# Gathering the experts' tokens from the fp32 stream, with a tenth expert unit loaded ahead

## What is computed

```python
h = layer_norm(DEEPNORM_ALPHA * h + mix, ln1_g[i], ln1_b[i])
...
t = h.reshape(b * l, d)
group_probs = jax.nn.softmax((t @ router_group_w).astype(jnp.float32) + router_group_b, axis=-1)
g_idx = jnp.argmax(group_probs, axis=-1)
exp_logits = jnp.einsum("td,gde->tge", t, router_expert_w).astype(jnp.float32) + router_expert_b
...
for gi in range(N_GROUPS):
    hid = (jax.nn.silu(jnp.einsum("td,edf->tef", t, expert_w_gate[gi]))
           * jnp.einsum("td,edf->tef", t, expert_w_up[gi]))
    hid = hid * combine[:, gi, :, None].astype(hid.dtype)
    y = y + jnp.einsum("tef,efd->td", hid, expert_w_down[gi])
```

## Time and profile before

| | us |
|---|---|
| median of 3 runs | 1086.28 |
| lowest, highest | 1086.09, 1087.94 |
| the profiled execution | 1088.23 |
| its span, first to last instruction | 1086.1 |
| PE busy in the span | 983.1 (91%) |
| DVE, ACT busy | 498.5 (46%), 354.2 (33%) |
| mean granted TensorE clock (share of full speed) | 0.964 |

### The profile page before, as it was taken

One profiled execution on the slowest core, in us unless ns is written; L12 is line 12 of the kernel. 1 busy time (PEld: TensorE's weight loads), 2 busy tenths in 40 slices (PEclk: granted clock), 3 DMA queues, 4 the chain that ended last, 5 costly groups with the idle time before them and its releaser, 6 DMA issues.

```text
span 1086.1 us, 14285 instructions
## 1 busy us (share of the span) xinstructions
PE 983.1 (91%) x6105; PEld 726.6 (67%) x6105; DVE 498.5 (46%) x777; ACT 354.2 (33%) x456; POOL 33.8 (3%) x51
## 2 busy tenths in 40 slices
PE   8989989999999984656877999999999989999996
PEld 7988776444456432213336887599998879889995
DVE  5973563271246102001038446355656565655554
ACT  3555303841022110001025436134343334434341
POOL 1400100021000000000000000000000000000000
PEclk9989999999999997878999999999999999999999
DMA  9724420452942999999995460445545344545520
GB/s 334 218 86 148 147 88 1 155 184 97 415 156 100 417 421 421 421 421 421 422 396 189 156 227 5 155 155 191 197 164 222 118 154 155 213 175 198 189 77 39
DMA packets 67126, 229.38 MB, mean 211 GB/s; under 512 B 4080, under 2 KB 5392, under 8 KB 54400
## 3 DMA queue, kind: packets, MB, share of 16 engines
q1 hardware_dynamic: 65216, 223.28, 54.2%
q0 software_dynamic: 1632, 5.26, 1.3%
q10 hardware_dynamic: 224, 0.07, 0.0%
HBM read 227.54 MB, written 1.05 MB: 210 GB/s over the span
## 4 chain that ended last, share of the span: by engine, by line
PE 74%; DMA 12%; DVE 9%; issue 2%; SPq 2%; ACT 1%; DVEq 0%; ACTq 0%
PE bank L1253 17%; PE bank L1264 16%; PE bank L1036 5%; DMA ring<-in_expert_w_up 5%; PE bank L676 4%; DMA arena<-in_expert_w_up 3%; PE bank L1162 3%; PE bank L665 3%; PE bank L960 3%; PE bank L929 3%; PE bank L1229 3%; PE bank L652 2%; DMA arena<-in_expert_w_down 2%; DVE arena L1744 2%; PE bank L1167 2%
## 5 line engine op out<-in xcount | busy, mean ns | idle before, releaser
L2174 DVE TENSOR_TENSOR w_lo<-ring,w_hi 128x2048 fp32r<-128x2048 f32 x76 | 170.6, 2288 | 97.4 <-ACT w_hi L1556 97.4
L1556 ACT ACTIVATE w_hi<-ring 128x2048 fp32r<-128x2048 f32 x76 | 141.1, 1909 | 87.9 <-PE bank L1264 86.9
L1253 PE MATMUL bank<-xT_hi,w_hi 128*128 128x256 f32 x512 | 143.8, 281 | 2.6 <-DVE xT_lo L2162 2.6
L1253 PE MATMUL bank<-xT_hi,w_lo 128*128 128x256 f32 x512 | 143.6, 280 | 0.0
L1253 PE MATMUL bank<-xT_lo,w_hi 128*128 128x256 f32 x512 | 143.2, 280 | 0.0
L1264 PE MATMUL bank<-w_hi,hidden_lo 128*128 128x512 f32 x256 | 99.9, 390 | 0.0
L1264 PE MATMUL bank<-w_lo,hidden_hi 128*128 128x512 f32 x256 | 99.8, 390 | 0.0
L1264 PE MATMUL bank<-w_hi,hidden_hi 128*128 128x512 f32 x256 | 99.6, 389 | 0.0
L1253 PEld LDWEIGHTS bank<-xT_hi,w_hi 128*128 128x128 f32 x512 | 96.1, 188 | 3.5 <-issue 3.0
L1253 PEld LDWEIGHTS bank<-xT_lo,w_hi 128*128 128x128 f32 x512 | 96.4, 188 | 0.5
L1253 PEld LDWEIGHTS bank<-xT_hi,w_lo 128*128 128x128 f32 x512 | 95.9, 187 | 0.0
(11 more groups left out here) (489 smaller groups left out, 1621.5 us busy)
## 6 DMA issues: line engine op xcount, KB each, us to landing
ring<-in_mlp_w_up SPq DMA_DIRECT2D x32, 1024.0 KB, 6.6
ring<-in_mlp_w_down SPq DMA_DIRECT2D x32, 1024.0 KB, 6.3
ring<-in_w_in SPq DMA_DIRECT2D x22, 1024.0 KB, 7.6
ring<-in_expert_w_down SPq DMA_DIRECT2D x22, 1024.0 KB, 19.7
ring<-in_expert_w_gate SPq DMA_DIRECT2D x16, 1024.0 KB, 15.4
ring<-in_expert_w_up SPq DMA_DIRECT2D x16, 1024.0 KB, 17.4
arena<-in_expert_w_gate SPq DMA_DIRECT2D x15, 1024.0 KB, 12.8
arena<-in_expert_w_up SPq DMA_DIRECT2D x15, 1024.0 KB, 14.8
```

The lines of the kernel that those rows point to most:

```text
L1253: last = mm(B[4 + (2 * j + pr) % 4][:, cc * SEQ:(cc + 1) * SEQ], w_[:, k * 512 + c * P:k * 512 + (c + 1) * P], x_[:, k, 0:SEQ], start=(k = ...
L1556: act(whi[:, n % 2, half], slot(u)[:, half], ACT.Copy).then_inc(S("split_hi"), 1)
L2174: tt(wlo[:, u % SLOTS, half], slot(u)[:, half], f32(whi[:, n % 2, half]), ALU.subtract).then_inc(S("split_lo"), 1)
```

## The change

- The gather reads X0 itself, in fp32, through a view with a step of 8 elements (`xhatT`); `hiX`, `loX`, `rounded`, `low_part` and the wait for `h1_low` are gone. `sel` and `sel_spill` are plain fp32. Of the matmuls in each gather 16 fp32 ones are left, with the same columns.
- A third unit is loaded once: unit 1 now takes all of X1, unit 2 lies in X2 and the start of `xT` and waits for the last output projection. All later units move down by one slot. Units 0 to 9 are now loaded ahead; unit j waits for unit j - 7 from j = 10 on.
- One `keep_going(1)` (an fp32 product of 512 columns whose result nobody reads) ahead of the rank products is removed.
- In a fallback for more overfull experts, which these inputs don't enter, X1 takes X0's place (that part of the diff is left out here).

```diff
--- before.py
+++ after.py
@@ -225,13 +225,10 @@
     wr, rbias = cube(arena[:, 18496:18496 + KD * 36], KD), arena[:, 18784:18820]
-    hiX = parts("h1_hi", "X1", 0, NT * D).rearrange("p (i k c) -> p i k c", i=NT, k=KD)
-    loX = parts("h1_lo", "xT", 0, NT * D).rearrange("p (i k c) -> p i k c", i=NT, k=KD)
+    xhatT = X0[:, :, :].rearrange("p i (c k) -> p i k c", k=KD)
     taken["arena"] = 0
-    sel = cube(parts("select", "arena", 0, NT * PAIR), NT)
-    reg(NT * PAIR)
-    sel_spill = cube(parts("select_spill", "arena", taken["arena"], NT * SPILL), NT)
-    reg(NT * SPILL)
+    sel = cube(reg(NT * PAIR), NT)
+    sel_spill = cube(reg(NT * SPILL), NT)
     selw = cube(reg(NT * PAIR), NT)
     selw_spill = cube(reg(NT * SPILL), NT)
     xs = cube(reg(KD * PAIR), KD)
@@ -327,20 +324,22 @@
     FIRST = MOE_UNITS + 2
     SPILLED = QUADS
     ORDER = [0, 1, SPILLED] + list(range(2, QUADS))
-    once = (params[:, :, :].rearrange("p a d -> p (a d)"), nc.alloc_sbuf_tensor_at("X1_X2", [P, UNIT], F32, offset=placed["X1"] + 4 * NT * D)[:, :])
+    ONCE = 3
+    assert placed["xT"] == placed["X2"] + 4 * NT * D == placed["X1"] + 4 * 3 * NT * D
+    once = [params[:, :, :].rearrange("p a d -> p (a d)"), X1[:, :, :].rearrange("p a d -> p (a d)"), nc.alloc_sbuf_tensor_at("X2_xT", [P, UNIT], F32, offset=placed["X2"])[:, :]]
     spare = [arena[:, SPARE + a * UNIT:SPARE + (a + 1) * UNIT] for a in range(3)]
-    FIRST_USE = [0, 5, 6, 7, 8, 2, 1, 3, 4]
+    FIRST_USE = [0, 5, 6, 7, 8, 9, 1, 3, 2, 4]
     def moe_at(s_, j):
         if s_ is None:
-            return MOE_SLOTS + j if j < 2 else (j - 2) % MOE_SLOTS
+            return MOE_SLOTS + j if j < ONCE else (j - ONCE) % MOE_SLOTS
         return j % MOE_SLOTS
     def moe_slot(s_, j):
         m = moe_at(s_, j)
-        return once[m - MOE_SLOTS] if m >= MOE_SLOTS else spare[m - 3] if 3 <= m < 6 else ring[:, {6: 3}.get(m, m), :]
+        return once[m - MOE_SLOTS] if m >= MOE_SLOTS else spare[m - 2] if 2 <= m < 5 else ring[:, (m + 1) % MOE_SLOTS if m < 2 else 3 * (6 - m), :]
     def moe_unit(s_, q):
@@ -491,17 +490,19 @@
             if s_ is not None:
                 sp.wait_ge(S("moe_unit"), total(s_, FIRST, MOE_UNITS, max(0, j - MOE_SLOTS + 1)))
-            elif j >= MOE_SLOTS + 2:
+            elif j >= MOE_SLOTS + ONCE:
                 sp.wait_ge(S("moe_unit"), j - MOE_SLOTS + 1)
             elif j == 0:
                 sp.wait_ge(S("gate_out"), 8)
                 sp.wait_ge(S("stream_made"), 2)
             elif j == 1:
                 sp.wait_ge(S("four_psum"), 4)
+            elif j == 2:
+                sp.wait_ge(S("mixed"), 4)
             elif j in (5, 6, 7):
                 sp.wait_ge(S("mix_psum"), 4)
             else:
-                of = U_TWO - 4 + (8, 2, 3, 4).index(j)
+                of = U_TWO - 4 + (8, 9, 3, 4).index(j)
                 sp.wait_ge(S(freed[of][0]), freed[of][1])
             for a, src in loads:
                 sp.dma_start(moe_slot(s_, j)[:, a:a + src.shape[1]], src).then_inc(S(f"moe_in{moe_at(s_, j)}"), 16)
@@ -514,7 +515,7 @@
                 flag = sp.value_load(ovi[0:1, 0:1], min_val=0, max_val=1)
                 expert = sp.value_load(ovi[0:1, 1:2], min_val=0, max_val=NG * NE - 1)
             for part in range(6 if q < SPILLED else 2):
-                if moe_unit(None, q) + part > MOE_SLOTS + 1:
+                if moe_unit(None, q) + part >= MOE_SLOTS + ONCE:
                     moe_load(None, moe_unit(None, q) + part, moe_loads(q, part) if q < SPILLED else spill_loads(expert, part))
         with sp.If(flag):
             with sp.Fori(0, PASSES - 1) as s_:
@@ -979,7 +980,6 @@
         carry(1)
         pe.wait_ge(S("router_dve"), 1)
         carry(0)
-        keep_going(1)
         pe.wait_ge(S("router_dve"), 3)
         of = lambda i: member[:, i].rearrange("p g e -> p (g e)")
         mm(B[4][:, 0:32], C("strict"), of(0), start=True, stop=True)
@@ -1001,8 +1001,7 @@
                     gathered(s_, gather_index(s_, p, 0))
                 for kk in range(2):
                     for i in range(NT):
-                        for m, x_ in enumerate((hiX, loX)):
-                            last = mm(B[(5, 6, 7, 5)[b]][:, kk * PAIR:(kk + 1) * PAIR], x_[:, i, 2 * b + kk, :], sel[:, i, :], start=(i == 0 and m == 0), stop=(i == NT - 1 and m == 1))
+                        last = mm(B[(5, 6, 7, 5)[b]][:, kk * PAIR:(kk + 1) * PAIR], xhatT[:, i, 2 * b + kk, :], sel[:, i, :], start=(i == 0), stop=(i == NT - 1))
                 last.then_inc(S("xs_psum"), 1)
         def gather_spill():
@@ -1011,8 +1010,7 @@
             for n in range(2):
                 for c in range(4):
                     for i in range(NT):
-                        for m, x_ in enumerate((hiX, loX)):
-                            last = mm(B[6 + n][:, c * P:(c + 1) * P], x_[:, i, 4 * n + c, :], sel_spill[:, i, :], start=(i == 0 and m == 0), stop=(i == NT - 1 and m == 1))
+                        last = mm(B[6 + n][:, c * P:(c + 1) * P], xhatT[:, i, 4 * n + c, :], sel_spill[:, i, :], start=(i == 0), stop=(i == NT - 1))
                 last.then_inc(S("xs_psum"), 1)
         def moe_landed(s_, j):
@@ -1020,8 +1018,8 @@
             m = moe_at(s_, j)
             if m >= MOE_SLOTS:
                 return pe.wait_ge(S(f"moe_in{m}"), 32)
-            main, per = 32 * len(range(m + 2, FIRST, MOE_SLOTS)), 32 * len(range(m, MOE_UNITS, MOE_SLOTS))
-            pe.wait_ge(S(f"moe_in{m}"), total(s_, main, per, 32 * ((j - (2 if s_ is None else 0)) // MOE_SLOTS + 1)))
+            main, per = 32 * len(range(m + ONCE, FIRST, MOE_SLOTS)), 32 * len(range(m, MOE_UNITS, MOE_SLOTS))
+            pe.wait_ge(S(f"moe_in{m}"), total(s_, main, per, 32 * ((j - (ONCE if s_ is None else 0)) // MOE_SLOTS + 1)))
         def up_quad(s_, q):
@@ -1130,7 +1128,6 @@
                     down_quad(s_, q)
             scatter(s_, order[-1], False, True)
-        pe.wait_ge(S("h1_low"), 2)
         keep_going(1)
         experts(None, ORDER)
         pe.wait_ge(S("over_made"), 1)
@@ -1486,18 +1483,11 @@
         warm_sqrt()
         deviation(5, slice(1, 3))
-        def rounded(i):
-
-            sc.wait_ge(S("xhat"), i + 1)
-            act(hiX[:, i], X0[:, i, :].rearrange("q (p k) -> q k p", k=KD), ACT.Copy).then_inc(S("h1_round"), 1)
-
-        rounded(0)
         for b in (0, 2):
             sc.wait_ge(S("four_psum"), 4 + b + 1)
             for k in (2 * b, 2 * b + 1):
                 last = act(xs[:, k, :], B[4 + b][:, (k % 2) * SEQ:(k % 2 + 1) * SEQ], ACT.Identity, scale=by_feature["ln1_g"][:, k:k + 1], bias=by_feature["ln1_b"][:, k:k + 1])
             last.then_inc(S("turned_act"), 1)
-        rounded(1)
         sc.wait_ge(S("router_dve"), 2)
         act(gd, gd, ACT.Exp).then_inc(S("router_act"), 1)
         sc.wait_ge(S("router_dve"), 4)
@@ -1948,13 +1938,6 @@
                 last = ts(xs[:, k, :], B[4 + b][:, (k % 2) * SEQ:(k % 2 + 1) * SEQ], by_feature["ln1_g"][:, k:k + 1], by_feature["ln1_b"][:, k:k + 1], ALU.mult, ALU.add)
             last.then_inc(S("turned_dve"), 1)
-        def low_part(i):
-
-            dve.wait_ge(S("xhat"), i + 1)
-            dve.wait_ge(S("h1_round"), i + 1)
-            tt(loX[:, i], X0[:, i, :].rearrange("q (p k) -> q k p", k=KD), f32(hiX[:, i]), ALU.subtract).then_inc(S("h1_low"), 1)
-
-        low_part(0)
         dve.wait_ge(S("router_in"), 16 * (NG + 5))
         dve.wait_ge(S("router_psum"), 1)
         for i in range(NT):
@@ -1987,7 +1970,6 @@
         line(tt(both, oh1, oh2, ALU.add))
         spread = lambda out, vals: [tt(out[:, i], oh[:, i, :].unsqueeze(2).broadcast_to([P, NG, NE]), vals[:, i, :].unsqueeze(1).broadcast_to([P, NG, NE]), ALU.mult) for i in range(NT)][-1]
         spread(member, both).then_inc(S("router_dve"), 1)
-        low_part(1)
         line(tt(w2, top2, top1, ALU.subtract))
         dve.nop().then_inc(S("router_dve"), 1)
         dve.wait_ge(S("router_dve"), 3)
@@ -2008,7 +1990,7 @@
             dve.wait_ge(S("sel_made"), pair_made(s_, p))
             for i in range(NT):
                 w_ = weight[:, i].rearrange("p g e -> p (g e)")[:, 8 * p:8 * p + 8].unsqueeze(2).broadcast_to([P, 8, CAP])
-                last = tt(cube(selw[:, i, :], 8), cube(f32(sel[:, i, :]), 8), w_, ALU.mult)
+                last = tt(cube(selw[:, i, :], 8), cube(sel[:, i, :], 8), w_, ALU.mult)
             last.then_inc(S("sel_weighed"), 1)
         select(0)
@@ -2062,7 +2044,7 @@
         red(spill_w, tmp, AX.X, ALU.add).then_inc(S("weighed"), 1)
         dve.wait_ge(S("weighed"), 2)
         for i in range(NT):
-            last = ts(selw_spill[:, i, :], f32(sel_spill[:, i, :]), spill_w[:, i:i + 1], None, ALU.mult)
+            last = ts(selw_spill[:, i, :], sel_spill[:, i, :], spill_w[:, i:i + 1], None, ALU.mult)
         last.then_inc(S("sel_weighed"), 1)
         def quad(s_, q):
```

6 lines of the change are left out of this document (3 added, 3 removed).

## The result

| | before | after |
|---|---|---|
| median of 5 runs, us | 1087.94 | 1093.16 |
| lowest, highest | 1086.09, 1089.28 | 1092.90, 1093.83 |
| span of the profiled execution, us | 1086.1 | 1091.1 |

The ratio is 1.005, with an interval of 1.0038 to 1.0063: slower by 5.2 to 5.4 us. I had forecast 1090.4 us, that is 4.1 us slower on a median of 1086.28, and a range up to 1092.6. The direction and the mechanism were right.

What follows compares the result with a forecast made beforehand. The expert stage was taken as bound by its weight transfers. Shift of first down products, -1.6 + 3.33 + 3.53 = +5.26 us, less 1.14 slack, gives +4.1 on 1086.28: 1090.4 us, range 1086.0 to 1092.6.

Steps and rivals of the forecast that it cites:

- The gap and the slack: Transfers ahead of unit 11: the tenth unit's lead becomes a gap; the stage's end shifts as first down products, less 1.14 us.
- later waits don't bind: Expert stage behind unit 11: unit 13 and later units find enough transfers queued, 10 to 15 us, to cover their waits.
- Slow load against free step: PE's weight loads in both gathers: the 32-byte step slows them (1090.4 us, chance 0.50) or costs nothing (1086.6 us, 0.38).
- The size of the load: Both gathers: a stepped load takes 0.225 us (bounds 0.20 to 0.26), adding 3.33 us to the gather, 3.53 to the spill gather.
- The saving ahead of the gather: Router's end: without the rounded and low parts and one `keep_going`, the path ahead of the gather is 1.6 us shorter.
- The base: Whole time: the 4.1 us shift is added to a median of 1086.28 us, 1.95 us below the profiled execution.
- Half clock: Third rival: a half-clock stretch of about 3.4 us on the gather or spill gather adds 1.7 us, 1092.1 us; chance 0.06.
- Free step: First rival: the step costs PE's weight load nothing, spill gather 3.7 us, 1086.6 us in all; chance 0.38.
- Faster: Second rival: both gathers cost no more than now, leaving saving and slack, -2.7 us, 1083.5 us; chance 0.06.

Runs made afterwards that it cites:

- e1: The changed kernel, but the gather reads the stream's features at a step of 1 element instead of 8 (wrong feature order): 1086.03 us, ratio 0.9984.
- e3: The changed kernel, but the gather reads at a step of 2 fp32 elements (8 bytes) instead of 8 (wrong feature order): 1087.29 us, one execution.
- e11: The changed kernel's fp32 gather with nine units loaded ahead, both gathers reading side by side one fp32 copy that ACT writes in the weights' order: 1089.7 us, ratio 1.0014.
- e10: The changed kernel with the spill gather moved from ahead of the first down products to just ahead of the spilled expert's up products: 1095.77 us, ratio 1.0073.
- e2: The changed kernel's fp32 stepped gather, but with the nine units loaded ahead and the slots of the kernel before: 1093.04 us, ratio 1.0045.
- e9: The kernel before without the `keep_going` ahead of the ranks; ACT scales the transposed stream first, GpSimd makes both low parts: 1089.69 us, ratio 1.0016.

## Why the prediction was too low

| counted from the end of the output projection, us | before | after | e1 | e3 | e11 | e10 |
|---|---|---|---|---|---|---|
| first down products end | 39.60 | 45.96 | 41.05 | 41.26 | 41.04 | 39.38 |
| last unit lands | 236.38 | 241.57 | 236.86 | 237.06 | 237.9 (estimate) | 243.14 |
| last scatter ends | 244.73 | 251.61 | 245.20 | 245.40 | 247.64 | 251.49 |

**The gap and the slack: right.** "Shift of the end = shift of those products - 1.14 us" gives +5.22 for the changed kernel, and +5.19 was measured; +0.31 and +0.52 for e1 and e3, measured +0.48 and +0.68. It fails for e10, where the first down products are no longer what is late. My sentence that "later waits don't bind" was right for this change, whose transfers run on at 418 to 424 GB/s from 384 to 412 us, and no more: it was worked out for PE's order as it stood, and e10 changes that order.

**Slow load against free step: right, by analogy with two other engines.** ACT's and DVE's rows did tell what PE does. The Trainium skill's SBUF — State Buffer, section Specifications (TRN2), asks for two accesses to a line of 16 bytes; steps of 4 and 8 bytes have them and cost next to nothing, 16 and 32 have not and cost double: the traces agree. The Trainium skill's TensorE: Matmul & The Clock Gate, section LDWEIGHTS, gives the time by the columns alone, and no step above 8 bytes here agrees with it.

**The size of the load: the first of two terms that failed.** "I take twice, 0.225 us with a little for the hand-over." The rows of the spill gather's products after:

```profile
L1013 PE MATMUL bank<-arena,X x32: 401/402/502, 346.7 to 354.2; 128*128 128x128 f32 x32
```

With the last one's 0.40 us off, (7.83 - 0.40) / 31 = 0.240 us from load to load, 2.2 times the 0.110 us without a step. That is 0.015 us in each of 62 intervals, 0.93 us. Another 0.33 us lies in the first and last records, which grew too: I had kept 0.38 and 0.28 us. So the gather cost +4.02 instead of +3.33 and the spill gather +4.10 instead of +3.53, together 1.26 us more than the sum had. The 0.240 lay inside my bounds, 0.20 to 0.26.

**The saving ahead of the gather: right.** 1.6 was taken, with 1.5 to 1.8. The gather starts at 17.95 instead of 19.70, 1.75 us earlier. With it the first down products: -1.75 + 4.02 + 4.10 = +6.37, and +6.36 was measured.

**The base: the second term that failed.** I added to 1086.28, the median of three runs. The medians of the kernel before in the later groups were 1087.17 to 1087.94. This is 0.9 to 1.7 us, as much as the load, and the range had 0.3 us for it at its lower end and nothing at its upper. With the measured load and my base the sum is 1091.5, with my load and a base of 1087.94 it is 1092.0, both inside the range; with both, 1087.9 + 5.2, it is 1093.1, and 1093.16 was measured. The profiled execution had shown it: it lay 1.95 us over the median to which I added. That the sum now fits so well is in part luck, for two things that it doesn't have cancel in the traces: half clock on the last down products after (+1.70), and half clock in the second block before (1.39 us, gone after).

**Half clock: the size was right, the place was not.** I had such a stretch on a gather at 1.7 us. Both gathers ran at full clock (1.00 from 328 to 356 us). It fell on the last down products, which took 1.7 us more (5.37 for 3.67); in the stretches of the changed kernel the clock reads

```profile
557.00:559.00 2.00, 2.00 (x12) 0.54 (x8) 0.00 (x0) 0.00 (x0) 0.00 (x0) 0.50 1.06 388
```

where 553 to 555 had 1.00, with PE busy for 0.66 us of the two. In the kernel before, PE was about as idle ahead of these products (busy for 0.75 us of the two from 549 to 551) and the clock stayed at 1.00, so I can't say what brings it on.

**The rivals.** Free step: refuted by the spill gather, as named (7.83 and not 3.7 us). With the step taken away it is what e1 shows, 1086.03 us. Faster: refuted; the fp32 gather costs 7.17 us even side by side.

## What to carry over

Where a stage is bound by transfers that wait for slots, one number rules an edit: how much later the releasing products may end before the queue runs dry, here 1.14 us. One more slot buys nothing while a later release is what is late (e2), and moving work away from one release loaded it on another (e10). Before an operand is read in place instead of from a copy, look at its step in bytes: from 16 bytes on a weight load cost double here, every time; a copy made once beside other work (e11) is cheaper than that. And put the spread of the runs into the range, at both ends, even where the median looks exact.

Of the kernels that keep the weights' order, none came out faster than the kernel before. e11 and e9 come nearest, at ratios of 1.0014 and 1.0016; only e11's interval reaches down to 1.

## What the hardware showed

- PE's loads of 128 fp32 columns cost nearly the same at a step of 4 and of 8 bytes (starts 0.110 and 0.119 us apart, records of 192 and 196 ns) and about double at 16 and 32 bytes (0.232 to 0.240 us, 330 to 335 ns). In fp32r, of which only 4 and 32 bytes were run, it is 0.110 us against records of 337 ns.
- A stream of 1 MB transfers, of which two thirds (gate and up) came in pieces of 2 KB, ran at 393 to 399 GB/s, all in pieces of 8 KB at 421, and an issue on SP's queue took 2.5 us instead of 0.43.
- A subtraction of 128 x 1024 on GpSimd held up VectorE's operations with two inputs for its whole length (two such operations took 1.32 and 2.77 us, where 0.17 is usual), and the one with one input beside it not at all (0.16 us).
- Eight products of the second block's first projection took 3.53 us at half clock and 2.13 us at full clock, in executions of kernels that are the same there.
